# One kernel of two blocks: the layers' entry inside block 1's output projection, banded add and row maximum in one instruction, keys' norms ahead of the queries'

## The chip, the cores and the metric

One core of one Trainium2 chip. The metric is the device time of one execution in microseconds (us), median of several. Engines: PE (TensorE, matmuls), ACT (ScalarE), DVE (VectorE), POOL (GpSimd), SP (SyncE, which issues most DMAs).

## The reference

512 tokens of width 1024 go through one `first_block` and two layers of `second_block`, all in float32:

```python
def first_block(x, ...):
    proj = rms_norm(x, norm_w) @ w_in                    # split into dn_qkv, dn_z, dn_b, dn_a, swa_*, gates
    qkv = silu(causal_depthwise_conv(dn_qkv, conv_w))    # 4 heads of 128
    dq = l2_normalize(dq) * HEAD_DIM ** -0.5
    dk = l2_normalize(dk)
    o_dn = gated_delta_rule_chunked(dq, dk, dv, g, beta) # chunks of 64 tokens
    y_dn = (rms_norm(o_dn, dn_norm_w) * silu(dn_z)) @ w_branch_dn
    # o_swa: softmax attention over 3 dilated windows (128,1), (512,4), (2048,16), merged by their log sums
    y_swa = (o_swa * silu(swa_z)) @ w_branch_swa
    return x + (sigmoid(g_dn) * y_dn + sigmoid(g_swa) * y_swa) @ w_out
def second_block(x, ...):                                # for each of 2 layers
    x = x + 0.5 * swiglu(rms_norm_2(x, ffn1_norm), ffn1_w_in, ffn1_w_out)
    # then: mix of three attentions, cross attention, second swiglu, norm
```

In the delta rule, `lower = strict(kb @ k^T) * decay` needs only the keys, and (I + lower) is inverted; the queries enter `a_intra` and the state's steps.

## The kernel before

`program` runs `block1_program` (0 to 780 us) and then `layers_program` (780 to 3002 us). Each is one `nc.Block()` with the instructions of each engine written out by hand in a function of its own; engines meet through semaphores, and a block ends with a barrier of all engines. Activations lie transposed: features over the partitions, the 512 tokens along the free axis (`xT`, 8 tiles of 128x512, named residual in the rows).

A float32 product is made of three matmuls of rounded halves (`three_mm`, L374 to L376): high x high, low x high, high x low. SP streams weight strips of 512 KB (8 tiles of 128x128) into a ring of four (`load_strip`, L188); ACT rounds a strip to its high half (`split_strip_act`, L362), DVE subtracts for its low half (`split_strip_dve`, L368). An activation's halves are made by `h_high_act` (ACT, L463, multiplied by the gain) and `h_low_dve` (DVE, L470).

Three places matter here.

*Block 1's output projection.* Eight strips of `w_out`, one for each tile n of the residual. For strip n + 2, ACT's loop (end of its function) waits for strip n on PE (`strip_done`) and makes the high half, DVE the low half; then DVE adds bank n into the residual tile n (L2844, counted by `x_done`). SP loads the residual back between the first strips. Then comes the barrier.

*The layers' entry.* Behind the barrier SP loads the first four strips of `ffn1_in` (`ffn_sp`). ACT issues the DMAs of the gains (L1494), loads its table (L1498), and makes high halves 0 to 2, the high half of strip 0, high halves 3 to 7, and that of strip 1; DVE follows with the low halves in the same order. ACT's squares of the eight residual tiles (L1526) come next; POOL adds them for the norm, which is applied behind the first matmuls.

*Block 1's delta rule, prologue.* `renorm_qk` lists eight norms, queries 0 to 3 and keys 0 to 3 (one per head): ACT squares a tile (`renorm_square`, L1882), PE sums it over the partitions with a matmul by ones (`renorm_sum`, L1899, banks 2 and 3 in turn), ACT takes logarithm and exponential (`renorm_root`, L1889 and L1892, two buffers), DVE scales (`renorm_scale`, L1906). PE has other work in between: the projection `attention_z` (four pieces of six matmuls), `gate_rows` (L2288, rows of decay and beta for a tile of tokens) and `keys_times("kk", t)` (L2293). DVE prepares the decays: `gate_blocks` (L2685, L2689), masks (L2695), "expo" (L2703), "kk_decay" and "LT" (L2711, L2714). From the first triangular step on (DVE L2722, PE L2331), PE and DVE take turns over four token tiles and the levels of the inversion.

*Block 1's windows.* 16 units (4 heads x 4 token tiles), each with three segments, one per window. `attn_pe_steps` makes the scores (L847), `attn_dve_steps` (`maxima`) adds the band to each segment (L976) into the unit's scores and takes the row maximum, negated, over all of them (L987); ACT takes the exponential (L917); PE transposes the result (L859), ACT copies it (L928), PE multiplies by the values (L873). The layers' attentions have the form of add and maximum in one instruction (L965).

## Time and profile before

| | |
|---|---|
| median of 3 runs | 3003.11 us (3001.58 to 3004.96) |
| profiled execution, its own time | 3003.86 us, span 3002.1 us |
| PE busy | 2893.7 us (96%) |
| DVE busy | 1464.8 us (49%) |
| ACT busy | 1097.6 us (37%) |
| POOL busy | 223.5 us (7%) |
| mean granted TensorE clock | 0.987 |

The span runs from the first to the last instruction of the profiled execution. Busy shares are averages over stages with different limits. In a row of the timeline, the bracket names the idle time ahead of an instruction and what ended it; in a row of waits, the first name is who waited, the second for whom.

### The profile page before, as it was taken

How to read it: one execution, taken by the hardware profiler on the slowest of the kernel's cores; microseconds unless marked ns; L12 is line 12 of the kernel's file. 1: busy time of each engine (PE TensorE's matmuls, PEld its weight loads, DVE VectorE, ACT ScalarE, POOL GpSimd, SP SyncE). 2: the span in 40 equal slices, each digit the busy share in tenths (PEclk: the TensorE clock that was granted, in tenths of full speed). 3: DMA queues.
4: the chain of work that ended last, by engine and by line, in shares of the span. 5: the costliest groups of instructions: out<-in, count | busy, mean ns of one | idle time of the engine just before them, and what ended most of it. 6: DMA issues, size and time to landing. Idle time of an engine off the chain costs nothing.

```text
span 3002.1 us, 36222 instructions
## 1 busy us (share of the span) xinstructions
PE 2893.7 (96%) x13458; PEld 2317.8 (77%) x13458; DVE 1464.8 (49%) x2042; ACT 1097.6 (37%) x1784; POOL 223.5 (7%) x166
## 2 busy tenths in 40 slices
PE   8899999899899999999999999999999999999998
PEld 5688777688788887577788888888886677788887
DVE  5673386543344433655454443544335555454432
ACT  4422344433333223656342322323224655433221
POOL 0000000000100022000220003100021001110011
PEclk9999999999999999999999999999999999999999
DMA  3201211024223323010212332222322111122332
GB/s 121 66 22 40 84 64 57 22 84 133 78 98 98 107 97 109 21 56 25 96 64 98 98 102 94 91 97 93 107 83 101 42 50 42 64 91 98 98 106 76
DMA packets 68363, 238.06 MB, mean 79 GB/s; under 512 B 10272, under 2 KB 12448, under 8 KB 67616
## 3 DMA queue, kind: packets, MB, share of 16 engines
q1 hardware_dynamic: 66240, 227.87, 23.0%
q10 hardware_dynamic: 2016, 8.77, 0.8%
q8 instruction: 67, 1.10, 0.2%
q14 instruction: 40, 0.33, 0.0%
HBM read 234.51 MB, written 2.10 MB: 79 GB/s over the span
## 4 chain that ended last, share of the span: by engine, by line
PE 68%; DVE 3%; ACT 2%; issue 1%; DMA 0%; DVEq 0%; ACTq 0%
PE bank L374 19%; PE bank L376 19%; PE bank L375 19%; PE bank L847 3%; PE bank L873 2%; PE bank L653 2%; PE bank L859 2%; PE bank L626 1%; ACT L_probs L917 1%; DVE L_scores L965 0%; PE bank L1460 0%; PE bank L226 0%; ACT L_h_hi L1598 0%; PE bank L1403 0%; DVE L_area L1781 0%
## 5 line engine op out<-in xcount | busy, mean ns | idle before, releaser
L374 PE MATMUL bank<-L_h_hi,L_w_hi 128*128 128x512 f32 x1776 | 704.3, 397 | 13.5 <-DVE L_weight_ring_low L368 9.8
L376 PE MATMUL bank<-L_h_hi,L_weight_ring_low 128*128 128x512 f32 x1776 | 693.0, 390 | 0.0
L375 PE MATMUL bank<-L_h_lo,L_w_hi 128*128 128x512 f32 x1776 | 693.0, 390 | 0.0
L362 ACT CAST L_w_hi<-L_weight_ring 128x1024 fp32r<-128x1024 f32 (+2 forms) x292 | 326.1, 1117 | 908.9 <-PE bank L376 901.9
L368 DVE TENSOR_TENSOR L_weight_ring_low<-L_weight_ring,L_w_hi 128x1024 fp32r<-128x1024 f32 (+2 forms) x292 | 393.8, 1349 | 377.9 <-ACT L_w_hi L362 377.7
L374 PEld LDWEIGHTS bank<-L_h_hi,L_w_hi 128*128 128x128 f32 x1776 | 334.4, 188 | 89.6 <-issue 15.4
L375 PEld LDWEIGHTS bank<-L_h_lo,L_w_hi 128*128 128x128 f32 x1776 | 334.6, 188 | 74.5 <-issue 5.8
L376 PEld LDWEIGHTS bank<-L_h_hi,L_weight_ring_low 128*128 128x128 f32 x1776 | 334.5, 188 | 70.2
L374 PE MATMUL bank<-L_act_hi,L_w_hi 128*128 128x512 f32 x704 | 273.9, 389 | 0.0
L375 PE MATMUL bank<-L_act_lo,L_w_hi 128*128 128x512 f32 x704 | 273.9, 389 | 0.0
L376 PE MATMUL bank<-L_act_hi,L_weight_ring_low 128*128 128x512 f32 x704 | 273.9, 389 | 0.0
L374 PE MATMUL bank<-B_h_hi,B_w_hi 128*128 128x512 f32 x480 | 197.7, 412 | 5.2 <-ACT B_arena L2569 1.8
L375 PE MATMUL bank<-h_low,B_w_hi 128*128 128x512 f32 x480 | 188.8, 393 | 0.0
L376 PE MATMUL bank<-B_h_hi,B_weight_ring_low 128*128 128x512 f32 x480 | 188.7, 393 | 0.0
L545 DVE TENSOR_TENSOR L_up<-bank,L_rstd 128x512 f32<-128x512 f32 x88 | 60.8, 691 | 246.0 <-PE bank L376 246.0
L368 DVE TENSOR_TENSOR B_weight_ring_low<-B_weight_ring,B_w_hi 128x1024 fp32r<-128x1024 f32 (+1 forms) x94 | 106.5, 1133 | 137.9 <-ACT B_w_hi L362 135.5
L873 PEld LDWEIGHTS bank<-L_area,L_probsT 128*128 128x128 f32 x960 | 131.0, 192 | 43.3 <-issue 28.0
L375 PEld LDWEIGHTS bank<-L_act_lo,L_w_hi 128*128 128x128 f32 x704 | 132.2, 188 | 27.5
L376 PEld LDWEIGHTS bank<-L_act_hi,L_weight_ring_low 128*128 128x128 f32 x704 | 132.2, 188 | 27.4
L374 PEld LDWEIGHTS bank<-L_act_hi,L_w_hi 128*128 128x128 f32 x704 | 132.2, 188 | 27.3
L362 ACT CAST B_w_hi<-B_weight_ring 128x1024 fp32r<-128x1024 f32 (+1 forms) x94 | 91.6, 975 | 147.9 <-PE bank L376 145.7
L211 POOL TENSOR_TENSOR L_squares_sum<-residual 128x512 f32<-128x512 f32 x8 | 10.0, 1252 | 1584.2 <-DVE residual L576 983.6
(319 smaller groups left out, 3881.7 us busy)
## 6 DMA issues: line engine op xcount, KB each, us to landing
L_weight_ring<-ffn_in SPq DMA_DIRECT2D x176, 512.0 KB, 3.3
L_weight_ring<-ffn_out SPq DMA_DIRECT2D x64, 704.0 KB, 4.0
B_weight_ring<-w_sqk SPq DMA_DIRECT2D x24, 512.0 KB, 3.3
B_weight_ring<-w_dn SPq DMA_DIRECT2D x16, 512.0 KB, 3.4
B_weight_ring<-w_gate SPq DMA_DIRECT2D x16, 512.0 KB, 3.3
L_weight_ring<-w_sna_qk SPq DMA_DIRECT2D x16, 512.0 KB, 3.3
L_weight_ring<-w_mix_out SPq DMA_DIRECT2D x16, 512.0 KB, 3.3
B_weight_ring<-w_sv SPq DMA_DIRECT2D x12, 512.0 KB, 3.3
```

The lines of the kernel that those rows point to most:

```text
L362: e.copy(hv.high(at)[:, 0:width], sh.ring[:, at % RING, 0:width]).then_inc(hv.w_hi_done, 1)
L368: e.tensor_tensor(hv.low(at)[:, 0:width], sh.ring[:, at % RING, 0:width], hv.high(at)[:, 0:width].bitcast(F32), ALU.subtract).then_inc(hv. ...
L374: e.matmul(out, a_hi, b_hi, start=start, stop=False)
L375: e.matmul(out, a_hi, b_lo, start=False, stop=False)
L376: return e.matmul(out, a_lo, b_hi, start=False, stop=stop)
L545: e.tensor_tensor(hv.up[:, :], sh.banks[2 * j + 1][:, :], sh.rstd[:, :], ALU.mult)\
L626: e.matmul(banks[sum_banks[b % len(sum_banks)]][:, 0:width], ones[0:kn, :], jb.sq[0:kn, b, 0:width], start=True, stop=True).then_inc(jb.su ...
L653: mm = e.matmul(bank[r0:r0 + rn, 0:job["width"]], w[:, off:off + rn], rhs, start=(i == 0 and m == 0), stop=(i == len(job["parts"]) - 1 and ...
L847: e.matmul(banks[b][:, 0:nk], q, k, start=True, stop=True).then_inc(at_.scored, 1)
L859: mm = e.transpose(banks[b][:, i * P:(i + 1) * P], at_.p[:, u % 2, kt * P:(kt + 1) * P], ident[:, :])
L873: mm = e.matmul(banks[at_.ob[ob]][:, c0:c0 + unit["dv"]], at_.pt[:, u % 2, i * P:(i + 1) * P], v, start=(i == 0), stop=(i == len(vs) - 1))
L917: e.activation(at_.p[:, u % 2, 0:nk], src, ACT.Exp, bias=at_.nm[:, s:s + 1], accum_out=at_.sums[:, s:s + 1]).then_inc(at_.exped, 1)
```

## The change

It has three parts.

*Entry.* `layers_program` becomes a generator: it lays out its tiles first (in memory that block 1 uses too, and at places that are free during the output projection), hands an `Entry` to `block1_program`, and goes on when block 1 is done. Block 1's functions then issue, inside the output projection: on SP the loads of the first two `ffn1_in` strips, into two places of their own, `first_strip` and `second_strip`; on ACT the gains' DMAs and the table, high halves 0 to 6 and those of the two strips; on DVE low halves 0 to 3 and those of the two strips. High half 7 and low halves 4 to 7 stay behind the barrier; the ring there begins with strips 2 and 3.

*Windows.* The banded add of a segment is a `tensor_tensor_reduce`, which writes the segment's maximum too; the row maximum is then taken over three numbers.

*Delta rule.* The keys' norms come first and the queries' after them, with the queries' sums in bank 7. PE's, ACT's and DVE's work is written in another order; PE waits for all eight norms only ahead of turn TT.

```diff
@@ Halves: the splits read a strip here
+    def raw(self, sh, at):
+        return self.ahead_raw[at] if at in self.ahead else sh.ring[:, at % RING, :]
...
-def ffn_sp(e, seen, sh, at, w_in, w_out):
+def ffn_sp(e, seen, sh, at, w_in, w_out, ahead=0):
+    if ahead:
+        seen.free(sh.strip_done, ahead)
+        for i in range(ahead, 4):
+            load_strip(e, seen, sh, at + i, w_in(i // 2, i % 2))
...
@@ attn_dve_steps, maxima
-                e.tensor_tensor(at_.sc[:, u % 2, c:c + n], banks[b][:, 0:n], bias, ALU.add)\
-                    .then_inc(at_.biased, 1)
+                e.tensor_tensor_reduce(at_.sc[:, u % 2, c:c + n], banks[b][:, 0:n], bias, 1.0, LOWEST, ALU.add,
+                                       ALU.max, at_.seg_mx[:, u % 2, i:i + 1]).then_inc(at_.biased, 1)
...
-            src = at_.sc[:, u % 2, 0:nk]
+            src = at_.seg_mx[:, u % 2, 0:len(unit["segs"])]
@@ layers_program
+            def loads_sp(self, e):
+                for i in range(2):
+                    e.dma_start(hv.ahead_raw[i], A["ffn1_in"][0, 0, i]).then_inc(sh.w_full[i], 16)
...
-                        table()
-                        e.wait_ge(gains_in, 16 * LAYERS)
-                        for k in range(KT):
-                            h_high_act(e, sh, g("ffn1"), hv.h_hi_done, hv.h_hi[:, k, :], k)
-                            if k == 2:
-                                split_strip_act(e, seen, sh, hv, 0, W_IN)
-                        split_strip_act(e, seen, sh, hv, 1, W_IN)
+                        h_high_act(e, sh, g("ffn1"), hv.h_hi_done, hv.h_hi[:, KT - 1, :], KT - 1)
...
-                        e.wait_ge(gains_in, 16 * LAYERS)
-                        for k in range(KT):
+                        for k in range(LOW_AHEAD, KT):
                             h_low_dve(e, seen, sh, hv, g("ffn1"), k)
-                            if k == 2:
-                                split_strip_dve(e, seen, sh, hv, 0, W_IN)
-                        split_strip_dve(e, seen, sh, hv, 1, W_IN)
@@ block1_program, PE
-                for j in range(8):
-                    renorm_sum(e, seen, sh, jb, j)
-                    if j == 3:
-                        attention_z(0, 3)
-                    if j in (4, 5):
-                        gate_rows(j - 4)
+                e.wait_ge(z_done, 1 + NH)
+                attention_z(0, 0)
+                e.wait_ge(conv_done, 3 + 3 * NH)
+                norm_sum(0)
+                norm_sum(1)
+                attention_z(0, 1)
+                gate_rows(0)
+                norm_sum(2)
+                attention_z(0, 2)
+                norm_sum(3)
+                gate_rows(1)
+                attention_z(0, 3)
                 e.wait_ge(gn_dve, 7)
...
+                    if turn == TT:
+                        e.wait_ge(jb.done, 2 + 8)
@@ block1_program, ACT
+                square(0)
+                square(1)
+                for j in range(4):
+                    root(j)
+                    square(j + 2)
+                decays(0)
+                decays(1)
+                for j in (4, 5):
+                    root(j)
+                    square(j + 2)
+                decays(2)
+                decays(3)
+                root(6)
+                root(7)
...
-                for n in range(KT - 2):
-                    e.wait_ge(sh.strip_done, seen.ready(sh.strip_done))
-                    split_strip_act(e, seen, sh, hv, V_FIRST + 68 + n + 2, KT * P)
+                entry.gains_act(e)
+                e.preload_act_table_set("natural_log_exp_and_others")
+                for n in range(KT - 1):
+                    if n < KT - 2:
+                        e.wait_ge(sh.strip_done, seen.ready(sh.strip_done))
+                        split_strip_act(e, seen, sh, hv, V_FIRST + 68 + n + 2, KT * P)
+                    if n == 1:
+                        entry.ready(e)
+                    if n == 4:
+                        entry.strip_act(e, 0)
+                    if n == 5:
+                        entry.strip_act(e, 1)
+                    if n > 0:
+                        e.wait_ge(sh.x_done, 2 + n)
+                        entry.high_act(e, n - 1)
@@ block1_program, DVE, output projection
+                    if n == 0:
+                        entry.ready(e)
+                    if 0 < n <= LOW_AHEAD:
+                        entry.low_dve(e, n - 1)
+                    if n == 5:
+                        entry.strip_dve(e, 0)
+                    if n == 6:
+                        entry.strip_dve(e, 1)
```

How the instructions stand on the engines, at three places (line numbers behind L are those of each kernel's own file).

ACT at the end of block 1 (L369 of the changed kernel and L362 of the one before are the same split, L475 and L463 the high half of a tile of h). Before:

```order
L362 CAST B_w_hi<-B_weight_ring 128x1024 x6
L2152 UNCONDITIONAL_BRANCH
L1490 UNCONDITIONAL_BRANCH
L1494 DMA L_gains<-gains 128x71 x2
L1498 ACT_TABLE_LOAD
```

In the changed kernel:

```order
L1340 DMA L_gains<-gains 128x71 x2
L2660 ACT_TABLE_LOAD
L369 CAST B_w_hi<-B_weight_ring 128x1024 x2
L475 ACTIVATE L_h_hi<-residual,L_gains 128x512
...
L369 CAST L_w_hi<-L_first_strip 128x1024
L475 ACTIVATE L_h_hi<-residual,L_gains 128x512
L369 CAST B_w_hi<-B_weight_ring 128x1024
L369 CAST L_w_hi<-L_second_strip 128x1024
L475 ACTIVATE L_h_hi<-residual,L_gains 128x512 x3
```

The gains, the table, seven high halves and two splits of the layers now stand between the splits of `w_out`.

PE in the delta rule's prologue, from the fifth sum of squares before (L1899), with the rows of gates (L2288) and the keys' products (L2293), to the first triangular step (L2331):

```order
L1899 MATMUL bank<-B_squares,shared_consts 128x512
L2288 MATMUL bank<-B_arena,shared_consts 128x512 x2
L1899 MATMUL bank<-B_squares,shared_consts 128x512
L2288 MATMUL bank<-B_arena,shared_consts 128x512 x2
L1899 MATMUL bank<-B_squares,shared_consts 128x512 x2
L2293 MATMUL bank<-B_arena 128x128 x8
L2288 MATMUL bank<-B_arena,shared_consts 128x512 x4
L2293 MATMUL bank<-B_arena 128x128 x8
L2331 MATMUL bank<-shared_consts,B_arena 128x128 x16
```

And in the changed kernel, where the same four are L1939, L2329, L2334 and L2387:

```order
L1939 MATMUL bank<-B_squares,shared_consts 128x512
L2334 MATMUL bank<-B_arena 128x128 x8
L1939 MATMUL bank<-B_squares,shared_consts 128x512
L2329 MATMUL bank<-B_arena,shared_consts 128x512 x2
L1939 MATMUL bank<-B_squares,shared_consts 128x512
L2329 MATMUL bank<-B_arena,shared_consts 128x512 x2
L2334 MATMUL bank<-B_arena 128x128 x8
L1939 MATMUL bank<-B_squares,shared_consts 128x512
L2387 MATMUL bank<-shared_consts,B_arena 128x128 x16
```

Four sums now stand behind the place where all eight were done, on both sides of the keys' products.

DVE in the same stretch, before (L1906 the scaling by a norm, L2703 "expo", L2685 and L2689 `gate_blocks`, L2711 and L2714 the decayed products):

```order
L2695 TENSOR_TENSOR B_arena<-B_consts,B_gate_numbers 128x512 x4
L1906 SCALAR_TENSOR_TENSOR B_arena<-B_arena,B_job_rstd 128x512 x8
L2703 TENSOR_TENSOR B_arena<-bank,B_arena 128x512 x2
L2685 TENSOR_TENSOR B_arena<-B_consts,B_gate_numbers 128x512
L2689 TENSOR_TENSOR B_arena<-shared_consts,B_gate_numbers 128x512
L2685 TENSOR_TENSOR B_arena<-B_consts,B_gate_numbers 128x512
L2689 TENSOR_TENSOR B_arena<-shared_consts,B_gate_numbers 128x512
L2711 TENSOR_TENSOR B_arena<-bank,B_arena 128x512
L2714 TENSOR_TENSOR B_arena<-bank,B_arena 128x512
L2711 TENSOR_TENSOR B_arena<-bank,B_arena 128x512
L2714 TENSOR_TENSOR B_arena<-bank,B_arena 128x512
```

In the changed kernel (L1946 the scaling):

```order
L2806 TENSOR_TENSOR B_arena<-bank,B_arena 128x512
L2809 TENSOR_TENSOR B_arena<-bank,B_arena 128x512
L2806 TENSOR_TENSOR B_arena<-bank,B_arena 128x512
L2809 TENSOR_TENSOR B_arena<-bank,B_arena 128x512
L1946 SCALAR_TENSOR_TENSOR B_arena<-B_arena,B_job_rstd 128x512 x2
L2784 TENSOR_TENSOR B_arena<-bank,B_arena 128x512 x2
L2806 TENSOR_TENSOR B_arena<-bank,B_arena 128x512
L2809 TENSOR_TENSOR B_arena<-bank,B_arena 128x512
L2806 TENSOR_TENSOR B_arena<-bank,B_arena 128x512
L2809 TENSOR_TENSOR B_arena<-bank,B_arena 128x512
L1946 SCALAR_TENSOR_TENSOR B_arena<-B_arena,B_job_rstd 128x512 x2
L2820 TENSOR_TENSOR B_arena<-B_arena,B_consts 128x512 x2
```

The scalings, eight in a row before, stand in four places: four keys' around the first two exponents, two queries' ahead of the second two, two at the end.

## Rows read from the trace of the kernel before

**Rows 1.** The page, part 1: busy time, share of the span, instructions per engine.
```profile
PE 2893.7 (96%) x13458; PEld 2317.8 (77%) x13458; DVE 1464.8 (49%) x2042; ACT 1097.6 (37%) x1784; POOL 223.5 (7%) x166
```

**Rows 2.** Busy time by stretches; at the end granted clock, DMA share, GB/s.
```profile
core 0: us, PE busy (x) PEld busy (x) DVE busy (x) ACT busy (x) POOL busy (x), PEclk, DMA share, GB/s
...
351.00:355.00 4.00, 3.83 (x10) 3.04 (x11) 0.69 (x1) 1.38 (x3) 0.00 (x0) 0.57 0.31 117
2527.00:2531.00 4.00, 3.95 (x17) 3.30 (x18) 3.17 (x3) 0.73 (x1) 2.64 (x2) 1.00 0.29 111
735.00:780.00 45.00, 44.12 (x193) 35.87 (x192) 15.61 (x19) 8.00 (x8) 0.00 (x0) 1.00 0.29 100
780.00:795.00 15.00, 6.06 (x14) 4.79 (x15) 9.37 (x16) 11.58 (x18) 2.12 (x2) 0.66 0.42 145
```

**Rows 3.** Timeline, PE, from block 1 into the layers: start, duration, instruction, [idle before].
```profile
779.34 0.39 PE L376 MATMUL bank<-B_arena_rounded,B_weight_ring_low 128*128 128x512 f32 x1
788.94 0.77 PE L374 MATMUL bank<-L_h_hi,L_w_hi 128*128 128x512 f32 x1 [9.22 <-DVE L_weight_ring_low L368]
789.51 0.63 PE L375 MATMUL bank<-L_h_lo,L_w_hi 128*128 128x512 f32 x1
...
795.05 0.41 PE L376 MATMUL bank<-L_h_hi,L_weight_ring_low 128*128 128x512 f32 x1
```

**Rows 4.** Timeline, ACT and DVE, same stretch.
```profile
780.74 0.83 ACTq L1494 DMA_DIRECT2D L_gains<-gains  x2
...
784.71 1.95 ACT L463 ACTIVATE L_h_hi<-residual,L_gains 128x512 fp32r<-128x512 f32 x3 [1.61 <-DMA L_gains<-gains]
...
786.56 1.03 ACT L362 CAST L_w_hi<-L_weight_ring 128x1024 fp32r<-128x1024 f32 x1
...
779.76 0.69 DVE L2844 TENSOR_TENSOR residual<-bank,residual 128x512 f32<-128x512 f32 x1 [4.75 <-PE bank L376]
```

**Rows 5.** Timeline, ACT, DVE and SP, in the output projection.
```profile
763.44 1.05 ACT L362 CAST B_w_hi<-B_weight_ring 128x1024 fp32r<-128x1024 f32 x1 [4.38 <-PE bank L376]
...
764.53 1.23 DVE L368 TENSOR_TENSOR B_weight_ring_low<-B_weight_ring,B_w_hi 128x1024 fp32r<-128x1024 f32 x1 [3.62 <-ACT B_w_hi L362]
...
741.64 16.68 SPq L188 DMA_DIRECT2D B_weight_ring<-w_out  x4
```

**Rows 6.** Timeline, PE, behind two other short gaps.
```profile
351.17 0.61 PE L374 MATMUL bank<-B_h_hi,B_w_hi 128*128 128x512 f32 x1 [1.82 <-ACT B_arena L2569]
...
2527.05 0.50 PE L374 MATMUL bank<-L_h_hi,L_w_hi 128*128 128x512 f32 x1 [1.89 <-DVE residual L1791]
```

**Rows 7.** Groups of DVE by form: busy us, mean ns | idle before.
```profile
L987 DVE TENSOR_REDUCE B_neg_max<-B_arena 128x1 f32<-128x1280 f32 x4 | 5.9, 1486 | 0.1
...
L987 DVE TENSOR_REDUCE B_neg_max<-B_arena 128x1 f32<-128x1024 f32 x4 | 4.9, 1220 | 0.1
...
L987 DVE TENSOR_REDUCE B_neg_max<-B_arena 128x1 f32<-128x384 f32 x4 | 2.2, 553 | 0.1
...
L965 DVE DVE_READ_ACCUMULATOR2_ANT L_row_max<- 128x1 f32 x64 | 5.3, 82 | 0.0
...
L969 DVE TENSOR_SCALAR L_neg_max<-L_row_max 128x1 f32<-128x1 f32 x64 | 9.8, 154 | 2.2
```

**Rows 8.** Waits of PE, 385 to 600 us: us in total, times, longest.
```profile
PE bank L859 <- ACT B_arena L917: 8.2, 3, 3.6
...
PE bank L847 <- DVE B_arena L762: 3.9, 3, 2.6
```

**Rows 9.** Waits of DVE, 118 to 156 us.
```profile
DVE B_arena L1906 <- ACT B_job_rstd L1892: 8.9, 8, 1.9
...
DVE B_arena L2703 <- PE bank L2288: 1.5, 1, 1.5
...
DVE B_arena L2711 <- PE bank L2293: 1.2, 1, 1.2
```

**Rows 10.** Timeline, DVE, begin and end of the prologue's chain.
```profile
120.19 0.69 DVE L2685 TENSOR_TENSOR B_arena<-B_consts,B_gate_numbers 128x512 f32<-128x512 f32 x1
...
154.74 1.42 DVE L2722 TENSOR_TENSOR B_arena<-B_arena,B_consts 128x512 f32<-128x512 f32 x2
```

More of the change, by code:

```diff
@@ L413, in turn @@
             for part in range(2):
-                s = at + 2 * j + part
+                s = at + 2 * j + part + (0 if first else 4)
                 e.wait_ge(hv.w_lo_done, seen.ready(hv.w_lo_done))
@@ L1091, in layers_program @@
             hv = Halves(sc, ffn_memory, sh.ring_lo)
+        with ExitStack() as loads:
+            sc.sb("under_act_hi", 20, T, ctx=loads)
+            raw = [sc.sb("first_strip", 2 * T, ctx=loads)]
+            sc.sb("under_act_lo", 19, T, ctx=loads)
+            raw.append(sc.sb("second_strip", 2 * T, ctx=loads))
+            hv.ahead_raw = [r[:, :] for r in raw]
         jb = Jobs(sc, hv.tmp, hv.up, (2,))
@@ L1305, in strips_before, with gains_act, ready, high_act @@
                 seen.passed(w, 16 * len(range(i, at, RING)))
+        memory.close()
+        hv.ahead[0] = hv.a_hi[:, 20:22, :].rearrange("p a b -> p (a b)")
+        hv.ahead[1] = hv.a_lo[:, 19:21, :].rearrange("p a b -> p (a b)")
+        seen_act, seen_dve = Tally(credit), Tally(credit)
+        class Entry:
+            def loads_sp(self, e):
+                for i in range(2):
+                    e.dma_start(hv.ahead_raw[i], A["ffn1_in"][0, 0, i]).then_inc(sh.w_full[i], 16)
+            def gains_act(self, e):
+                for layer in range(LAYERS):
+                    e.dma_start(gains[:, layer, :], A["gains2"][layer]).then_inc(gains_in, 16)
+            def ready(self, e):
+                e.wait_ge(gains_in, 16 * LAYERS)
+            def high_act(self, e, k):
+                h_high_act(e, sh, gain(0, "ffn1"), hv.h_hi_done, hv.h_hi[:, k, :], k)
+            def low_dve(self, e, k):
+                h_low_dve(e, seen_dve, sh, hv, gain(0, "ffn1"), k)
+            def strip_act(self, e, i):
+                split_strip_act(e, seen_act, sh, hv, i, W_IN)
+            def strip_dve(self, e, i):
+                split_strip_dve(e, seen_dve, sh, hv, i, W_IN)
+        yield Entry()
         with nc.Block() as block:
@@ L1491, in _ @@
             def _(e):
-                seen = Tally(credit)
-                for layer in range(LAYERS):
-                    e.dma_start(gains[:, layer, :], A["gains2"][layer]).then_inc(gains_in, 16)
+                seen = seen_act
                 e.sem_inc(jb.rstd, 1)
@@ L1892, in renorm_root, with renorm_sum @@
     e.activation(jb.rs[:, j % 2, :], jb.rs[:, j % 2, :], ACT.Exp, scale=-0.5).then_inc(jb.rstd, 1)
-def renorm_sum(e, seen, sh, jb, j):
+def renorm_sum(e, seen, sh, jb, items, j):
     e.wait_ge(jb.squared, seen.ready(jb.squared))
-    e.wait_ge(jb.rstd, seen.free(jb.rstd))
-    e.matmul(sh.banks[2 + j % 2][:, :], sh.ones[:, :], sh.sq[:, j % 2, :], start=True,
+    e.wait_ge(jb.rstd, seen.free(jb.rstd) + ("bank" in items[j] and "bank" in items[j - 1]))
+    e.matmul(sh.banks[items[j].get("bank", 2 + j % 2)][:, :], sh.ones[:, :], sh.sq[:, j % 2, :], start=True,
              stop=True).then_inc(jb.summed, 1)
@@ L2247, in attention_z @@
                         mm.then_inc(sh.strip_done, 1)
-                e.wait_ge(z_done, 1 + NH)
-                for piece in range(3):
-                    attention_z(0, piece)
-                e.wait_ge(conv_done, 3 + 3 * NH)
                 def first_values(t, strips):
@@ L2501, in step, with decays @@
                     done[0] += 1
-                for t in range(TT):
+                def decays(t):
                     step("decay", t)
@@ L3007, in program @@
         stored = ctx.enter_context(nc.semaphore("stored"))
-        block1_program(nc, banks, xT, x_lo, const, A)
-        layers_program(nc, banks, xT, const, A, out, stored)
+        layers = layers_program(nc, banks, xT, const, A, out, stored)
+        block1_program(nc, banks, xT, x_lo, const, A, next(layers))
+        next(layers, None)
 def kernel(**inputs):
```

101 lines of the change are left out of this document (64 added, 37 removed).

## The prediction

> **What bounds the kernel now.** I read the page first: TensorE (PE) is busy 96% of the span, 2893.7 of 3002.1 us [rows 1]. So an edit pays only where PE stands still or runs at its lower clock, and I looked for these places next. The table by stretches shows the last strips of block 1's output projection with PE busy 44.12 of 45 us at full granted clock; the 15 us behind them hold 6.06 us of PE work at a granted clock of 0.66 [rows 2]. The other views are the timelines of the three places that the change touches and the lists of waits there.
>
> **The change part by part.** The sum is made against the profiled execution, 3003.86 us; that is 0.75 above the median of the runs, 3003.11.
>
> *Part A, the layers' entry.* What happens now: PE's last matmul of block 1 begins at 779.34 and its first of the layers at 788.94, after 9.22 us idle that ended with the low half of the first weight strip [rows 3]. In that gap, one after another: VectorE's (DVE's) last residual add, from 779.76; the barrier between the two programs; ScalarE's (ACT's) issue of the gains' DMA at 780.74; their landing, for which ACT waits until 784.71; three high halves; the first strip's split at 786.56; DVE's low half of it [rows 4]. The change puts all of that into the output projection, but for the last high half and the low halves 4 to 7. Does it fit there? In a steady strip of the projection ACT idles 4.38 us before its split, and DVE idles 3.62 us before its low half [rows 5]. Added per strip on ACT: one high half (1.95/3 = 0.65) and in two strips a split of 1.03 [rows 4], together 1.7 at most. Added on DVE: one low half of h, which I price like the 128x512 add at 0.69 [rows 4], or one of a strip, 1.23 [rows 5]. Both fit twice over; I cost the moved arithmetic at nothing, and its cover is this idle time. If that were gone, the strip's own split would come late and PE with it, by what is over 3.6 us in each strip. The DMAs count too: the gains' two are issued by ACT ahead of the projection, and the two strips' by SP, behind the eight strips of w_out. SP issues the last of these when a ring slot comes free, at 758.3 (741.64 + 16.68 [rows 5]), which leaves 6 us before ACT asks for the first new strip. On SP's queue nothing stands behind them; the ring of the layers then starts with strips 2 and 3, after the barrier as before.
>
> What stays between the programs: the last add (779.76 + 0.69 = 780.45), the barrier (ACT's first instruction behind it starts at 780.74 [rows 4]) and PE's own presets of semaphores. I take 781.45 for PE's first matmul: 0.7 us behind ACT's first, with bounds of 780.8 and 782.4. That is 7.5 us earlier than 788.94. PE then asks for one k-tile in three matmuls, some 0.7 us, and DVE makes low halves 4 to 7 at 0.69 each from 781.3, four tiles ahead of PE, so nothing waits there.
>
> Then the clock. After today's gap, 13 matmuls start 0.426 us apart (789.51 to 795.05 [rows 3]) where later ones take 0.227: with the first one, 2.9 us lost. Does a gap of 1.7 us still bring that? Two rows in the trace are near it: before 351.17 PE idled 1.82 us between dense matmuls, and the clock granted after it is 0.57; before 2527.05 it idled 1.89 us, and the clock stays at 1.00 [rows 2, 6]. The first case costs 1.6 us (eight matmuls 0.2 longer), the second nothing. I take the middle, 0.8, with both ends kept. Part A: -7.5 - 2.9 + 0.8 = **-9.6**, from -7.5 to -11.
>
> The Trainium skill bears on this (TensorE: Matmul & The Clock Gate, Part 1: The HAM clock gate): it says that the throttled state is the default, which activity releases, and that the number of matmuls at the low level differs between runs of one kernel. By it the stretch could come back whole behind a short gap too, and the sum would be worse by 2.1 us. Rows 6 show both outcomes for nearly equal gaps, which agrees with it.
>
> *Part B, block 1's sliding windows.* Sixteen units of three segments each. Now a segment is added to its band, and the row maximum is then taken over all 384 to 1280 elements: 0.553 to 1.486 us, four units of each size; 1280 and 1024 are the long ones [rows 7]. The change takes the maximum along with the addition and reduces three numbers per row instead. No row shows the fused form in block 1, but the layers use it: its read of the accumulator is 0.082 us, and a one-column instruction 0.154 [rows 7]; I count 0.12 per read with its spacing and 0.15 for the small reduction. So DVE saves 1.486 - 0.12 - 0.15 = 1.2 us of latency in a unit of 1280, 0.95 in one of 1024, and about 0.3 in one of 384. (Two reads in front of the last are hidden where DVE waits for PE's scores, and cost 0.24 where it does not.) In all, DVE loses some 8.6 us of work, but only what PE waits for is time. PE waits for the exponentials three times, 8.2 us in all, and three times for a query or key that DVE finishes, 3.9 us, of which 2.6 is one wait at the stage's start and the two others, 1.3 together, stand behind a reduction of 1280 [rows 8]. Of the three waits two follow a reduction over 1280 and one over 1024: 2 x 1.2 + 0.95 = 3.35. With the 1.3, less 0.25 for reads that are not hidden: **-4.4**. At the low end only one wait in three is shortened, -1; at the high end a half-clock stretch goes too, -7.
>
> *Part C, the delta rule's prologue.* Now all eight norms (four queries', four keys') run first; DVE scales each as ACT delivers it and waits 8.9 us in eight waits for ACT, then 1.5 and 1.2 us for PE's rows [rows 9]. The chain ends in the first triangular step on DVE, at 154.74 [rows 10], which PE waits for. From 120.19 to there DVE executes 32 operations of about 0.72 us (the last two of one line take 1.42 [rows 10]), 23 us; the other 11.6 are the waits of rows 9. So the floor of any new order is 120.2 + 23 = 143.2, which is 11.5 us earlier. The new order starts the norms' sums behind one piece of attention z instead of three, and needs only the keys' four before kk. I stepped the three engines' new lists by the durations of the trace (ACT 0.6 for each of logarithm, exponential and square; PE 0.86 for a sum; DVE 0.72): key 3 is scaled at 131.7 (ACT still delivers one norm per 1.7 to 2.5 us), gate blocks 2 and 3 end at 135.3, the first two tiles' decays at 138.2, the others' at 144.6; the last query's sum waits in the two-deep buffer until 144.3, so query 7 is scaled at 147.5, and the triangular step begins at 147.5. The same stepping of the old lists gives 154.7, as measured. **-7.3**, between -5 (another half-clock stretch and slower hops between engines) and -9. The wait that DVE keeps is that for query 7; all triangular steps stand behind it on DVE, and PE behind them, and this is what is late next. PE's matmuls are the same in number, so nothing is added.
>
> **Sum:** -9.6 - 4.4 - 7.3 = -21.3: the profiled execution would be 2982.6, and the median 0.75 lower, **2981.8**.
>
> **The rivals.**
> 1. *The clock takes its part back.* The short gap at the entry is followed by a stretch at half clock like that at 351.17, and a new one arises in the prologue, where PE now alternates between short sums and waits. For it: rows 2 and 6. Against it: 2527.05. Part A gives 8.8 or a little less, part C 5: total -18, **2985**. Chance 0.17.
> 2. *Part B is hidden.* The exponentials of the last units wait for scores anyway, and PE waits as long for the transposes behind them; only 1 us of 4.4 is left: -18, again **2985**. For it: DVE is not the engine that is busiest there, and the three waits also hold the exponential itself, which stays. Against it: the timeline shows each of the three exponentials starting right behind its reduction. Chance 0.13.
> 3. *The prologue's chain only moves its waits.* ACT holds the decays of two tiles ahead of roots 4 and 5; if the exponents come late, the queries' norms, now behind kk, hold up the first triangular step, and C gives 2 or less: -16, **2987**. Chance 0.08.
> 4. *Slower than before:* the entry's first strip lands late. ACT splits it in the projection ahead of the split of w_out's last strip, and executes in order: a late DMA holds that split, then DVE's low half, then PE. Point of decision: ACT asks at 764.5, and the last strip must be split and lowered (1.05 + 1.23 [rows 5]) before PE needs it at about 774.3, so landing up to 772 costs nothing, 14 us after issue. Behind that each microsecond costs one, and the kernel is slower than now only if the strip comes more than 35 us after issue (**3005** at 37 us). Against it: today the same load, issued behind the barrier, is there when ACT wants it at 786.56 [rows 4], under 6 us later, with three more beside it. Chance 0.02.
> 5. *The change does not do what it says.* A semaphore holds the early work until the barrier (for one, the gains land late), and A gives nothing: -12, **2991**. Chance 0.04.
>
> **How the numbers follow.** The forecast itself has 0.56: all three parts pay, in total -18.5 to -25. Its own range is 2978 to 2985. Cases 1 and 2 and their mixtures lie between 2983 and 2988. The low ends of all parts together would be 2976. So 2975.5 to 2989.5 holds a little over 8 in 10, leaving out cases 4, 5 and half of case 3. About 0.2% (6 us) is what a measurement of this kernel can tell from no change; faster than that means below 2997. Every case but 4 and some mixture of 3 and 5 lies below it: faster 0.94, the same 0.04, slower 0.02.
>
> **What would show each step.** A: PE's first matmul of the layers 1.5 to 2 us behind its last of block 1 (now 9.6), ACT's table load and gains' issue ahead of the projection's splits, PE's spacing in the projection unchanged; wrong if splits in the projection end PE's idle time, or if the granted clock behind the gap is near 0.66 for 6 us. B: reductions of 0.15 to 0.2 us and custom instructions with a read each, DVE in the attention some 8 us less busy, the three waits for exponentials together under 5.5 us; wrong if they stay at 8. C: the first triangular step about 147.5, seven of eight waits for ACT gone or short, and a last wait for query 7; wrong if it begins after 151. The prediction as a whole is wrong above 2990, and then I would look first at what the shorter gap does to the clock.

## The result, and the profile after

The changed kernel takes 2984.76 us (median of 5 runs, 2981.31 to 2986.87) against 3003.11 before (median of 5, 3001.46 to 3004.96): a ratio of 0.9937, 95% interval 0.9926 to 0.9948, or 18.4 us less. 2981.8 had been forecast, with a range of 2975.5 to 2989.5. The profiled execution took 2981.31 (span 2979.5), at the lower edge of the five.

The page, part 1, of the changed kernel, against [rows 1]:

```profile
PE 2887.5 (97%) x13458; PEld 2315.7 (78%) x13458; DVE 1453.0 (49%) x2090; ACT 1097.5 (37%) x1784; POOL 223.8 (8%) x166
```

PE's busy time is 6 us less with the same number of matmuls; DVE has 48 instructions more (the accumulator reads) and 12 us less work.

The entry, timeline of PE, against [rows 3]. PE now idles 1.8 us between the blocks' matmuls, where it idled 9.22, and the first matmul comes 2.19 us behind the last instead of 9.60. The releaser named is the second of DVE's presets, but PE's own sequencer was busy with its presets of semaphores until then (the version that follows, below, shows it):

```profile
766.72 0.39 PE L383 MATMUL bank<-B_arena_rounded,B_weight_ring_low 128*128 128x512 f32 x1
768.91 0.47 PE L381 MATMUL bank<-L_h_hi,L_w_hi 128*128 128x512 f32 x1 [1.81 <-DVEq L1705]
```

The moved work in the output projection, timeline of ACT and of DVE, against [rows 4, 5]:

```profile
750.83 1.05 ACT L369 CAST B_w_hi<-B_weight_ring 128x1024 fp32r<-128x1024 f32 x1 [3.76 <-PE bank L383]
751.78 1.05 ACT L369 CAST L_w_hi<-L_first_strip 128x1024 fp32r<-128x1024 f32 x1
752.73 0.72 ACT L475 ACTIVATE L_h_hi<-residual,L_gains 128x512 fp32r<-128x512 f32 x1
756.26 1.05 ACT L369 CAST B_w_hi<-B_weight_ring 128x1024 fp32r<-128x1024 f32 x1 [2.81 <-PE bank L383]
```

```profile
757.35 1.22 DVE L375 TENSOR_TENSOR B_weight_ring_low<-B_weight_ring,B_w_hi 128x1024 fp32r<-128x1024 f32 x1 [2.96 <-ACT B_w_hi L369]
758.49 0.68 DVE L2942 TENSOR_TENSOR residual<-bank,residual 128x512 f32<-128x512 f32 x1
759.09 1.22 DVE L375 TENSOR_TENSOR L_act_hi<-L_first_strip,L_w_hi 128x1024 fp32r<-128x1024 f32 x1
```

ACT still idles 2.81 to 3.76 us ahead of a split of `w_out`, DVE 2.96 ahead of its low half. The first strip of the layers is split right behind the projection's own split, without a wait for its DMA. From the first branch matmul to the last matmul of block 1 PE takes 175.12 us, and 175.18 before.

The prologue, waits of DVE and its timeline at the end, against [rows 9, 10]:

```profile
DVE B_arena L1946 <- ACT B_job_rstd L1932: 3.5, 3, 1.4
...
DVE B_first_values L2845 <- PE bank L2387: 1.6, 1, 1.6
...
DVE B_arena L2806 <- PE bank L2334: 1.0, 1, 1.0
```

```profile
145.62 0.69 DVE L1946 SCALAR_TENSOR_TENSOR B_arena<-B_arena,B_job_rstd 128x512 f32<-128x512 f32 x1 [1.16 <-ACT B_job_rstd L1932]
146.34 1.42 DVE L2820 TENSOR_TENSOR B_arena<-B_arena,B_consts 128x512 f32<-128x512 f32 x2
```

The first triangular step begins at 146.34 instead of 154.74; this execution as a whole was 0.5 us earlier by then (its first piece of attention z is at 117.85, not 118.35), so 7.9 us are gained. Query 7 is the last wait, as forecast, 1.16 us.

The windows, groups of DVE by form and waits of PE, against [rows 7, 8] (L872 and L860 here are L859 and L847 there):

```profile
L989 DVE DVE_READ_ACCUMULATOR2_ANT B_segment_max<- 128x1 f32 x48 | 4.0, 82 | 0.0
...
L1000 DVE TENSOR_REDUCE B_neg_max<-B_segment_max 128x1 f32<-128x3 f32 x16 | 2.5, 156 | 0.6
```

```profile
PE bank L872 <- ACT B_arena L941: 9.3, 13, 1.2
PE bank L872 <- ACT B_arena L930: 4.5, 3, 2.4
PE bank L860 <- DVE B_arena L774: 2.6, 1, 2.6
...
PE bank L860 <- DVE B_segment_max L989: 1.8, 1, 1.8
```

Two more waits of PE in the kernel before:

```profile
PE bank L859 <- ACT B_arena L928: 7.9, 13, 0.9
...
PE bank L847 <- DVE B_arena L976: 0.5, 1, 0.5
```

The reduction over three numbers takes 0.156 us and a read 0.082, near the prices taken (0.15; 0.12 with the spacing). PE's three waits for exponentials fell from 8.2 to 4.5 us. But its waits for ACT's copies of transposed blocks rose from 7.9 to 9.3. The wait for a bank that DVE has not yet read, 1.8 where it was 0.5, is no effect of the edit: the kernel before, profiled again, has 1.8 as well, and the last version below has 0.5. In the 7.7 us ahead of it the granted clock is 1.00 where the wait is 1.8, and 0.78 where it is 0.5: the slower PE arrives later and waits less.

### The profile page after: what moved, and what is told of

The parts are those of the page before. It is cut to its first block, busy times and chain, and to the rows that moved or that the text cites. A ratio compares the mean times of both kernels' runs of the same rounds, so it can differ in the third digit from the quotient of the medians.

```text
span 2979.5 us, 36258 instructions
## 1 busy us (share of the span) xinstructions
PE 2887.5 (97%) x13458; PEld 2315.7 (78%) x13458; DVE 1453.0 (49%) x2090; ACT 1097.5 (37%) x1784; POOL 223.8 (8%) x166
## 4 chain that ended last, share of the span: by engine, by line
PE 68%; DVE 3%; ACT 2%; issue 1%; DVEq 0%; ACTq 0%
PE bank L381 19%; PE bank L383 19%; PE bank L382 19%; PE bank L860 3%; PE bank L886 3%; PE bank L665 2%; PE bank L872 2%; PE bank L638 1%; ACT L_probs L930 1%; DVE L_scores L978 1%; PE bank L1512 0%; PE bank L227 0%; PE bank L1455 0%; DVE L_area L1821 0%; ACT L_h_hi L1642 0%
## 5 line engine op out<-in xcount | busy, mean ns | idle before, releaser
L383 PE MATMUL bank<-L_h_hi,L_weight_ring_low 128*128 128x512 f32 x1760 | 685.9, 390 | 0.0
L369 ACT CAST L_w_hi<-L_weight_ring 128x1024 fp32r<-128x1024 f32 (+2 forms) x290 | 324.1, 1118 | 910.2 <-PE bank L383 899.9
L886 PEld LDWEIGHTS bank<-L_area,L_probsT 128*128 128x128 f32 x960 | 131.9, 193 | 43.8 <-issue 28.4
L369 ACT CAST B_w_hi<-B_weight_ring 128x1024 fp32r<-128x1024 f32 (+1 forms) x94 | 91.6, 975 | 142.7 <-PE bank L383 142.6
```

Of the source, the lines that this page charges most:

```text
L369: e.copy(hv.high(at)[:, 0:width], hv.raw(sh, at)[:, 0:width]).then_inc(hv.w_hi_done, 1)
L383: return e.matmul(out, a_lo, b_hi, start=False, stop=stop)
L886: mm = e.matmul(banks[at_.ob[ob]][:, c0:c0 + unit["dv"]], at_.pt[:, u % 2, i * P:(i + 1) * P], v, start=(i == 0), stop=(i == len(vs) - 1))
```

## The experiments

Each kernel was compared with the kernel before on the same chip. Besides the time I read stages from the trace: the **prologue** (first piece of attention z to PE's first triangular step), the **delta rule** (the same start to the first matmul behind its last long wait), the **windows** (first scores to first branch matmul), and the **entry** (block 1's last matmul to the layers' first).

### One part alone

The first three are the kernel before with the diff's edits of one part. The entry alone:

```diff
+                entry.gains_act(e)
...
+                    if n == 4:
+                        entry.strip_act(e, 0)
...
+        layers = layers_program(nc, banks, xT, const, A, out, stored)
+        block1_program(nc, banks, xT, x_lo, const, A, next(layers))
```

> The kernel before with the entry alone moved into the output projection; the delta rule and the windows as before. Theory (the parts pay independently): from block 1's last matmul to the layers' first 2.2 us as in the changed kernel (9.6 before), a half-clock stretch of 1.4 us or none behind it instead of 2.9, prologue (first piece of attention z to first triangular step on PE) 37.2 as before, windows stage (first scores to first branch projection) 204.8 as before; time 8.7 to 10.2 below before. Rival (the early entry only pays where block 1 already runs ahead, or the clock takes it back whole): 5 or less below before.

Measured: 2993.52 us against 3003.66, ratio 0.9966 (0.9952 to 0.9979), 10.1 less. The entry's gap is 2.19 us and no half-clock stretch follows: the granted clock of the next 6 us is 1.00. The windows took 205.9 and the prologue 35.5, where 204.8 and 37.2 had been expected of code that this run leaves as it was.

```profile
783.40:789.40 6.00, 6.00 (x27) 4.94 (x28) 4.74 (x9) 4.56 (x10) 4.47 (x3) 1.00 0.49 175
```

The windows alone:

```diff
-                e.tensor_tensor(at_.sc[:, u % 2, c:c + n], banks[b][:, 0:n], bias, ALU.add)\
+                e.tensor_tensor_reduce(at_.sc[:, u % 2, c:c + n], banks[b][:, 0:n], bias, 1.0, LOWEST, ALU.add,
...
```

> The kernel before with the fused add and maximum alone. Theory (only the exponentials' three waits and DVE's lateness ahead of them count): windows stage 201.8 instead of 204.8, waits of PE for the exponentials 4.5 instead of 8.2, time 3 below before. Rival (all 8.6 us of DVE work saved turn up): 8 below. Rival (hidden): within 1 of before.

Measured: 3000.79 against 3003.66, ratio 0.9990 (0.9981 to 0.9999), 2.9 less. The windows took 202.0 us. PE's waits there are those of the changed kernel to a tenth:

```profile
PE bank L860 <- ACT B_arena L929: 9.3, 13, 1.2
PE bank L860 <- ACT B_arena L918: 4.5, 3, 2.3
```

So the shift from one wait to another belongs to this part and not to the others. Of the work that DVE saves (138.3 us busy in the stage before, 124.5 now, which is 13.8 and not the forecast's 8.6) a quarter shows in the time.

The delta rule's order alone:

```diff
-        renorm_qk = [dict(src=dn[:, 4 + i, :], scale=1.0, factor=HD ** -0.5 if i < 4 else 1.0) for i in range(8)]
+        renorm_qk = [dict(src=dn[:, 8 + i, :], scale=1.0, factor=1.0) for i in range(4)]
+        renorm_qk += [dict(src=dn[:, 4 + i, :], scale=1.0, factor=HD ** -0.5, bank=7) for i in range(4)]
...
```

> The kernel before with the delta rule's new order alone. Theory: prologue 29.3 us instead of 37.2, of which some 0.5 is given back in the turns behind it; time 7.4 below before. Rival (the turns were bound elsewhere and take it back): less than 4 below.

Measured: 2995.18 against 3003.66, ratio 0.9977 (0.9965 to 0.9989), 8.5 less by the medians (7 by the ratio). The prologue took 29.8 us, 7.4 less than in the profile before; the delta rule took 175.7, before 182.25, so in this pair of profiles the turns behind the prologue gave 0.9 back. In the mean they gave nothing back: 145.4 us in the four profiles with the old order, 145.5 in seven with the new.

The three parts' medians sum to 21.5, the whole change to 18.4. The intervals are 5 to 8 us wide each, so this is no sign of an interaction.

### Which half of the new order pays

```diff
-                for piece in range(3):
-                    attention_z(0, piece)
+                attention_z(0, 0)
...
-                    if j == 3:
-                        attention_z(0, 3)
+                    if j in (1, 2, 3):
+                        attention_z(0, j)
```

> The kernel before, with one part of the delta rule's new order alone: the sums of squares begin behind one piece of attention z instead of three, the queries still first. Theory (the start of the sums and the order keys first each pay a part): ACT's first logarithm 4.1 us behind the first piece (6.9 before, 4.2 in the changed kernel), prologue 2 to 3 us shorter than before, 5 longer than the changed kernel's. Rival A (all of the gain is the early start): prologue 29 to 30. Rival B (all is the order of the keys): prologue as before.

Measured: 3000.09 against 3002.51, ratio 0.9992 (0.9983 to 1.0000). ACT's first logarithm came 4.1 us behind the first piece, and the prologue took 33.5 us. DVE still waits for ACT in six places:

```profile
DVE B_arena L1906 <- ACT B_job_rstd L1892: 7.0, 6, 1.9
```

Against 37.2 in the two profiles of the kernel before this is 3.8 less, against 35.5 in the run of the entry alone, 2.1, and against 34.0 in the run of the windows alone, 0.5; but that last one had the granted clock at 1.00 in its first 7 us, and this run 0.77, like the other three (0.76). So at a like clock the early start gives 2 to 4 us in a single profile, and the keys' place in front (29.3) the other 4. Rival A falls. Rival B falls by this comparison at a like clock; the total time, 2.4 us less with an interval that ends at 1.0000, does not settle it.

### What is late next

```diff
-                scale(6)
-                scale(7)
-                e.wait_ge(jb.done, 2 + 8)
                 levels = k1("levels").rearrange("p (l i) -> p l i", l=LEVELS)
...
                 off_diagonal(0)
                 off_diagonal(1)
+                scale(6)
+                scale(7)
+                e.wait_ge(jb.done, 2 + 8)
```

> The changed kernel, but DVE scales queries 6 and 7 behind its first two triangular products instead of ahead of them. Theory (what is late next is DVE's wait for the last query, 1.2 us, and its own 0.7 us for query 6): the first triangular step on DVE at 143.9 instead of 146.3, on PE at 144.8 instead of 147.2; of these 2.4 us 1.5 or more stay in the time, since DVE otherwise waits 1.6 us for PE's first step. Rival (DVE is the bound in the turns, so work put there comes back whole): within 0.7 of the changed kernel.

Measured: 2984.04 us, ratio to before 0.9936 (0.9922 to 0.9949): by the time alone, no different from the changed kernel. The stage shows it nevertheless: the first triangular step on DVE begins at 143.56, on PE 26.8 us behind the first piece instead of 29.3, and the delta rule takes 171.4 us instead of 174.9 (172.6 to 175.7 in seven profiles with its old order of the last two queries), so the gain stays through the turns. DVE, timeline:

```profile
143.56 1.42 DVE L2817 TENSOR_TENSOR B_arena<-B_arena,B_consts 128x512 f32<-128x512 f32 x2
144.89 1.28 DVE L1946 SCALAR_TENSOR_TENSOR B_arena<-B_arena,B_job_rstd 128x512 f32<-128x512 f32 x2
146.25 0.69 DVE L2845 TENSOR_TENSOR B_first_values<-shared_consts,bank 128x512 f32<-128x512 f32 x1
```

Both scalings now run while PE makes its first step. What hides it between these two profiles: the windows took 203.3 us against 201.8, the stage ahead of them 98.6 against 97.1 (98.8 to 98.9 in the changed kernel's two later profiles), and the program from the first scores of the layers' attention to its end 1793.3 against 1789.9, all code that this edit does not touch. That 1.5 us or more would stay in the time, as expected, is therefore shown by the stage alone.

### How much of this is the clock

> The kernel before, unchanged, profiled once more. Theory (the granted clock behind a short gap differs from run to run of the same code): the prologue takes another time than the 37.2 us shown, between 34 and 37, the granted clock of 118 to 125 us being 0.76 or 1.00. Rival (the prologue's time follows from the code alone): 37.2 again within 0.3.

Measured: 3002.48 us. The prologue took 37.2 again, so what I expected of this run was wrong. The windows, however, took 208.5 instead of 204.8, at a mean granted clock of 0.94 instead of 0.96, with equal waits but one (the wait for a bank that DVE has not read, 1.8 instead of 0.5). That the prologue of this code varies is shown by the run with the windows' edit alone, which leaves the prologue's instructions as they were: 34.0, with the granted clock of 118 to 125 us at 1.00. Of the repeated kernel before, and of that run:

```profile
118.00:125.00 7.00, 7.00 (x21) 5.08 (x22) 5.37 (x11) 2.65 (x6) 0.00 (x0) 0.76 0.06 22
```

```profile
118.00:125.00 7.00, 6.11 (x22) 4.05 (x22) 5.40 (x10) 4.20 (x9) 0.00 (x0) 1.00 0.17 67
```

In the first, ACT's first logarithm comes 6.9 us behind the first piece, in the second 5.3. There is a second difference: both profiles of the kernel before have a wait of DVE for PE's rows, 1.5 us [rows 9] and 1.6; the runs of the entry alone and of the windows alone, with the same instructions in the prologue, have none. In the profiles of the kernel before, a stretch at half clock falls on these rows:

```profile
145.00:150.00 5.00, 3.73 (x5) 1.65 (x6) 3.33 (x6) 1.23 (x2) 0.00 (x0) 0.66 0.01 3
```

In the other two it comes some 6 us earlier, counted from the first piece (granted clock 0.53 in 141.0 to 144.6 us and in 140.6 to 144.2), while DVE has other work.

Does PE's idle time at the entry bring the stretch that follows it? Six matmuls into an unused bank, three ahead of the barrier and three behind:

```diff
+                for _ in range(3):
+                    e.matmul(banks[5][:, :], hv.high(0)[:, 0:P], hv.h_hi[:, 0, :], start=True, stop=True)
                 e.sem_inc(sh.strip_done, RING)
...
                     mm.then_inc(sh.strip_done, 1)
+                for _ in range(3):
+                    e.matmul(banks[5][:, :], hv.high(at + KT - 1)[:, 0:P], merged_hi[:, 0, :], start=True, stop=True)
```

> The changed kernel with six extra matmuls into a bank that nothing reads at that time, three behind block 1's last and three behind the barrier ahead of PE's presets, so that PE runs through most of the gap. Theory (the half-clock stretch behind the entry comes from PE's idle time): 60 matmuls from the layers' first on take 13.7 us instead of 15.3, the gap between the blocks' own matmuls stays 2.2 to 2.3, time 0.7 to 1.6 below the changed kernel. Rival (the stretch has nothing to do with the gap, or the barrier alone is gap enough): 15.3 again.

> The changed kernel, unchanged, profiled once more. Theory (behind a gap of 2.2 us the half-clock stretch comes in some runs and not in others): 60 matmuls from the layers' first on take 13.7 or 15.3 us; gap 2.2. The prologue may differ from 29.3 by a stretch as well.

> The kernel with six extra matmuls around the barrier, unchanged, profiled once more. Theory (PE's idle time brings the stretch): no stretch behind the entry again, 60 matmuls in 13.7 to 14.1 us. Rival (chance): 15.3 as in two of the three profiles without the extra matmuls.

> The changed kernel, unchanged, a third profile: as for the second, 13.7 or 15.3 us for 60 matmuls behind the entry.

> The kernel with six extra matmuls around the barrier, unchanged, a third profile: 13.7 to 14.1 us for 60 matmuls behind the entry by the theory, 15.3 at least once by the rival.

Measured: 2983.58 us with the extra matmuls, ratio to before 0.9936 (0.9923 to 0.9950). The single runs: 2983.53 and 2984.78 of the changed kernel, 2988.53 and 2984.00 of the one with extra matmuls. The gap between the blocks' own matmuls is 2.22 with them and 2.19 to 2.23 without, so they cost nothing there. The 60 records from the layers' first own matmul on took 15.3 us in the changed kernel's first profile and 14.0 in its second and third, and 14.0 in all three with extra matmuls (13.7 in the run of the entry alone; a record that is missing from a trace shifts this count by 0.23). Granted clock of the 6 us behind the layers' first matmuls, changed kernel, then its second profile:

```profile
769.00:775.00 6.00, 6.00 (x20) 4.75 (x21) 5.91 (x9) 4.22 (x9) 4.53 (x3) 0.72 0.51 176
```

```profile
773.00:779.00 6.00, 5.99 (x26) 4.63 (x26) 5.97 (x9) 4.25 (x9) 4.59 (x3) 1.00 0.49 176
```

Without extra matmuls the five profiles of this entry (three of the changed kernel, the entry alone, the queries late) have 0.72, 1.00, 1.00, 1.00 and 0.72; with them the three and that of the run below have 1.00 each. The five profiles of the old entry, with a gap of 9.5 to 9.8 us, all have a stretch, of 5 to 13 slow matmuls. This speaks for the theory but does not settle it: at two in five, four without a stretch would come about by chance once in eight times.

### The version that follows

Queries 6 and 7 late, PE's four presets issued by POOL, three extra matmuls ahead of the barrier and one behind it:

```diff
@@ layers_program, PE
-                e.sem_inc(sh.strip_done, RING)
-                e.sem_inc(sh.sum_mm, 2)
-                e.sem_inc(jb.summed, 2)
-                e.sem_inc(at_.pv_done, 2)
+                for _ in range(1):
+                    e.matmul(banks[5][:, :], hv.high(0)[:, 0:P], hv.h_hi[:, 0, :], start=True, stop=True)
@@ layers_program, POOL
                 e.sem_inc(raw_read, 2)
+                e.sem_inc(sh.strip_done, RING)
...
```

> The changed kernel with queries 6 and 7 scaled late, PE's presets of semaphores issued by POOL, three extra matmuls behind block 1's last and one behind the barrier. Theory: prologue 26.8 us, gap between the blocks 1.5 to 1.7 instead of 2.2, no half-clock stretch behind it; 3 to 5 us below the changed kernel. Rival (PE then waits for DVE's presets, or the clock spoils it): gap 2.2 again, 1 to 2 below.

Measured: 2980.91 us (2979.45 to 2983.73) against 3002.51, ratio 0.9926 (0.9912 to 0.9939): 21.6 less than before, 3.2 more than the change as given, though the two intervals overlap. The prologue took 26.0, in a profile with the granted clock at 1.00 in its first 7 us; the changed kernel has 28.4 in its one profile like that. PE, timeline at the entry:

```profile
766.76 0.39 PE L383 MATMUL bank<-B_arena_rounded,B_weight_ring_low 128*128 128x512 f32 x1
766.99 0.84 PE L2495 MATMUL bank<-B_arena_rounded,B_w_hi 128*128 128x512 f32 x3
768.20 0.49 PE L1403 MATMUL bank<-L_h_hi,L_w_hi 128*128 128x512 f32 x1 [0.38 <-PEq L2198]
768.52 0.40 PE L381 MATMUL bank<-L_h_hi,L_w_hi 128*128 128x512 f32 x1
```

The gap is 1.76 us, 0.43 less: what stood between the barrier and PE's first matmul were PE's own presets. With that, the next wait appears, PE for a low half of h:

```profile
PE bank L381 <- DVE L_h_lo L482: 0.5, 1, 0.5
```

To take that wait away, low halves 4 to 7 would have to be made in the projection too; it was not tried.

## Why the prediction was right

The forecast was 21.3 us less in the profile, 2981.8 in the median; 2984.76 was measured. The two profiled executions differ by 22.6, but only 19.6 of it lies in the three stages; most of the rest is code that no edit touches (1.7 between the delta rule and the windows, 1.3 behind the entry), so that this pair comes so near to 21.3 is in part luck. The stages, from all profiles with the old and all with the new code of each (four to nine of each, so that stretches at half clock average out; the mean of each side), give 9.2 for the entry, 6.7 for the prologue and 3.2 for the windows: 19.1 together, 2.2 less than forecast. All three parts pay, by the waits that the prediction named; each was priced somewhat too high.

- **Entry, forecast 9.6.** The start of PE was right: 2.19 us behind the last matmul, where 2.11 (781.45 less 779.34) was forecast; PE's presets are part of what is left. The moved arithmetic cost nothing, as its cover said: PE's spacing in the projection did not change. The choice of the middle between a stretch and none fits the five profiles, two with and three without; the profiled execution of the changed kernel is one with a stretch (seven matmuls 0.427 us apart). What was mis-sized is the 2.9 us for today's stretch: the profile before has 13 slow matmuls, the most of the five profiles of the old entry (5 to 13), and in the mean of all of them the clock gives back 1.7 us, not 2.1. The Trainium skill's sentence that was weighed there (TensorE: Matmul & The Clock Gate, Part 1: The HAM clock gate), that the number of slow matmuls differs between runs of one kernel, is said there of a kernel's start; the three profiles of the changed kernel show the same in its middle: 7, 0 and 0.
- **Prologue, forecast 7.3.** Stepping the lists gave 147.5 for the triangular step on DVE. 146.34 was measured, which is 146.8 counted from the same start, so 0.7 was too much waiting. The rest of the order came as stepped: key 3 scaled at 131.5 from the same start (forecast 131.7), the last query the last wait. But my price for "before", 37.2 us of prologue, was itself a profile with two half-clock stretches: the first puts off the first logarithm by 1.6 us, the second, where it falls, brings the 1.5 us of waiting for PE's rows, which the prediction took for a part of the old order. That the stepped old list met the measured 154.7 was in part luck. The mean of four profiles is 36.0, and 6.7 of gain is nearer the truth than 7.9. At a like clock it is less: 34.0 against 28.4 with 1.00 in the first 7 us, 35.5 against 29.3 to 29.8 with 0.76.
- **Windows, forecast 4.4.** This is the term that was mis-sized. The three waits for exponentials shrank by 3.7, a little more than the 3.35 forecast, since a read costs less than the 0.12 taken (last section). The step that failed is "the two others, 1.3 together, stand behind a reduction of 1280". They do, and they vanished; but PE then waits as long at the next place. Its transposes follow 0.65 us earlier, and the copy that frees the bank for the second four is queued on ACT behind a weight split. In the kernel before PE waits in two places, 0.64 and 0.51:

```profile
451.56 0.49 PE L847 MATMUL bank<-B_arena 128*128 128x128 f32 x2 [0.64 <-DVE B_arena L762]
...
453.22 0.55 PE L859 MATMUL bank<-shared_consts,B_arena 128*128 128x128 f32 x3 [0.51 <-ACT B_arena L928]
```

In the changed kernel it waits in one, 1.23; ACT and PE:

```profile
441.49 0.60 ACT L696 ACTIVATE B_job_squares<-bank 128x512 f32<-128x512 f32 x1 [1.68 <-PE bank L383]
...
441.98 1.04 ACT L369 CAST B_w_hi<-B_weight_ring 128x1024 fp32r<-128x1024 f32 x1
...
442.91 0.59 ACT L941 COPY B_arena<-bank 128x512 f32<-128x512 f32 x1
...
443.56 0.66 PE L872 MATMUL bank<-shared_consts,B_arena 128*128 128x128 f32 x4 [1.23 <-ACT B_arena L941]
```

That split stands behind the squares, which ACT begins when PE is done with the strip before, whatever DVE does. Rival 2 had named this mechanism, but for the last units; it acts at two earlier ones, and takes 1.4 us, so of the term of 1.3 nothing was left. The 3.2 of the mean holds one profile of 208.5 on the side before; at a like mean clock the stage gained 2.9 (204.8 to 201.8, at 0.96) and 2.5 (205.9 to 203.4, at 0.95).
- **The rivals.** Rival 1 (the clock) is at work in single runs, not in the mean: it moves the time of one execution by 1 to 4 us at each of several places. Rival 3 had the right place and the wrong size: the last query does hold up the first triangular step, by the 2.5 us that the run with queries 6 and 7 late took away, but part C gave 6.7 and not 2. Rivals 4 and 5 fell: the first strip is there when ACT asks, and the entry starts where it was said to.

## What to carry to other kernels

Where one program follows another behind a barrier, look for the idle time of each engine in the last stage of the first and put the second's loads, tables and splits there; they cost nothing as long as they fit that idle time, strip by strip, and what is left is the barrier and the engine's own presets. Shortening the work ahead of a wait gives only the distance to the next thing that the waiting engine needs, so follow that engine two instructions further, into the queue of whoever serves it, before counting the gain. And an edit of a few microseconds is better read from its stage in several profiles than from the total, since code that it does not touch moves by as much: from the layers' first 60 matmuls to the end the fourteen profiles took 2194 to 2204 us.

## What the runs showed of the hardware that was not expected

One code takes different times at the same place: the old prologue 34.0 to 37.2 us, the old windows 204.6 to 208.5, the first 60 matmuls behind the new entry 13.7 to 15.3. The records show the same instructions and other granted clocks: 0.76 or 1.00 in the prologue's first 7 us with a later stretch at half clock that falls in two places, 0.94 to 0.96 over the windows, 0.72 or 1.00 in 6 us behind the entry. The waits of PE in the windows, summed by their releasers, repeat to a tenth of a microsecond in most rows, and are the better measure of what an edit did; but one row of them, and one of DVE's in the prologue, came and went with the clock.

A fused add and maximum costs less than its two rows say. The forecast counted 0.12 us for each read of the accumulator. But where segments follow one another, the next one starts together with the read: two of 128x512 start 0.61 us apart, and the plain adds of the kernel before 0.60. The reduction starts 0.73 us behind the last fused instruction, and 0.71 to 0.73 behind the last plain add. DVE, in the kernel before and in the changed one:

```profile
445.12 1.28 DVE L976 TENSOR_TENSOR B_arena<-bank,B_arena 128x512 f32<-128x512 f32 x2
...
446.43 1.49 DVE L987 TENSOR_REDUCE B_neg_max<-B_arena 128x1 f32<-128x1280 f32 x1
```

```profile
435.67 0.69 DVE L989 CUSTOM_DVE_ANT_0 B_arena<-bank,B_arena 128x512 f32<-128x512 f32 x1
...
436.28 0.08 DVE L989 DVE_READ_ACCUMULATOR2_ANT B_segment_max<- 128x1 f32 x1
436.28 0.69 DVE L989 CUSTOM_DVE_ANT_0 B_arena<-bank,B_arena 128x512 f32<-128x512 f32 x1
...
437.01 0.16 DVE L1000 TENSOR_REDUCE B_neg_max<-B_segment_max 128x1 f32<-128x3 f32 x1
```

So a read adds some 0.01 us to a unit's chain, the last one too. A unit of 1280 saves 1.486 less 0.156, one of 1024 1.220 less 0.156; twice the one and once the other make the 3.7 by which the three waits shrank. The same price accounts for DVE's 13.8 us: the reductions shrank from 16.8 to 2.5, and 48 reads took about half a microsecond back.

And a preset of a semaphore on PE is not free: four of them, 0.15 us apart, with the first wait behind, held PE's first matmul until 768.91, 0.86 us behind the barrier (ACT's first activation starts at 768.34). Issued from POOL, they let it begin 0.43 us earlier, although one extra matmul stood ahead of it there.
